# Two fused transformer blocks on one core: state-free delta steps moved ahead, state-space half first in the output projection, layer norms per token tile

## The chip, the cores and the metric

One core of one Trainium2 chip. The metric is the device time in microseconds (us) of one execution of the whole program; lower is better. PE is the matrix engine (TensorE), DVE the vector engine, ACT the scalar engine, POOL GpSimd, SP the engine that issues the weight transfers.

## What is computed

Everything is float32, with 256 tokens of width 1024. Block 1 is attention, convolution and memory attention, then a mixture of 32 experts. Block 2 runs two recurrences, a state-space scan (SSD) and a gated delta rule (GDN), over 256 context tokens and then over the 256 latent tokens, in both directions and in chunks of 64, of which the kernel takes two at a time. The change touches the GDN scan and what comes after it:

```python
def gdn_step(s, inp):                       # per chunk; u, w from a triangular solve
    u_c, w_c, qk_c, qg_c, kd_c, dec_c = inp # these don't depend on the state s
    v_new = u_c - einsum("bhlk,bhkv->bhlv", w_c, s)
    o = einsum("bhlk,bhkv->bhlv", qg_c, s) + einsum("bhls,bhsv->bhlv", qk_c, v_new)
    s = s * dec_c[..., None, None] + einsum("bhlk,bhlv->bhkv", kd_c, v_new)
...
y = rms_norm(y_ssd * silu(z)) * norm_w_ssd
o = rms_norm(o_gdn) * norm_w_gdn * silu(gate)
mixed = concatenate([y, o], -1)                            # 256 x 2048
x = layer_norm(ALPHA * x + g1 * (mixed @ w_out), ln1_g, ln1_b)
h = x * (1 + sc2) + sh2
x = layer_norm(ALPHA * x + g2 * ((silu(h @ w_ffn_gate) * (h @ w_ffn_up)) @ w_ffn_down), ln2_g, ln2_b)
```

g1, sh2, sc2 and g2 are rows of a modulation product, silu(c) @ w_ada + b_ada; the FFN is 2816 wide.

## The kernel before

Each engine's program is written out by hand, and engines wait for each other by semaphores alone. Products go to eight PSUM banks of 128x512; `TileOrder` (L69) hands the banks out in program order (MAIN is 0 to 5, THREE 5 to 7), and a product that opens a bank waits until the engine that reads it has drained the bank's last tile. SP streams the weights in a fixed order through a ring of six 1 MB slots.

The delta rule is cut into phases. `delta_phases` (L109) gives their order, and `gdn_pe` (L580), `gdn_act` (L923), `gdn_dve` (L1147) and `gdn_pool` (L1485) each do their engine's part of a phase and yield its name. There are eight steps: 0 to 3 over the context, whose phases are dealt out between the experts by `mixed_schedule` (L139) from costs in `context_phases` (L121), and 4 to 7 over the latents, one after the other with nothing around them. The phases of a step:
- "rows": PE turns the keys (two tiles of 4 transposes), spreads the decay sums (L551 on), ACT copies them out and POOL masks.
- "gram": PE multiplies keys by keys (gKK) and for latents keys by queries (gQK), L591. DVE makes the masked matrix A from gKK (L1177), copies its 16x16 diagonal blocks (L1184), multiplies them into "spread" (L1191, which gives spread_ready), and then applies the mask to gQK (L1196).
- "rep": PE multiplies blk16 by spread (gRep, four products of 128x512, L614); ACT copies the four tiles (L952); POOL solves the 16x16 blocks in 15 dependent steps of two instructions (L1525, L1526) on Y and then expands Y into XT (eight instructions of 128x128, L1528), which gives XT_ready.
- "kS", "M", "u", "M2", "t", "w", "x", "v", "out": the products with the state and the solve. "M" waits for XT_ready (L621); "w" also holds go1, the queries by the state, whose scaling DVE does at L1207; "out" gives the outputs (go2, added by DVE at L1216) and the next state (gS, L1222 and L1223).
The phases rows, gram and rep of step m+1 lie between those of step m; for the first step of a sequence they stand ahead. Around the latent steps, at the phases in `MOD_PHASES` (L504), PE does a piece of the modulation product: `mod_sum` (L767, row at L771) and `mod_part` (L760, L2068), with ACT copying a part and DVE adding at L1349 (`modulate`).

`second_block_pe` (L696) runs the block in order: channels, SSD steps 4 to 7 (one loop, in each two gate tiles, L1921, and then the inner product, L754), the latent delta steps, 16+16 transposes of the rows y and o (L1915), the output projection `long_product("w2", ...)` (L806) from four weight units, 16 transposes of the normed rows h_ffn, then gate and up products of the FFN (tiles of 256 channels by 256 tokens, "fg0" the first), and `long_product("fd", ...)`. On DVE, `gated_y` (L1352) forms and squares the y rows, `normed_y` (L1362) scales a quarter of them, `o_squares` (L1376) measures an o tile; `residual` (L1423) adds a product tile to x and sums rows; `layer_norm` (L1434) works over both token tiles in one go: centre and square both, one root, then scale and shift each, with `modulated` (L1448) for h_ffn. POOL multiplies x by ALPHA once h_ffn is there.

```python
for phase in ("kS", "M", "rows", "u", "M2", "gram", "t", "w", "rep", "x", "v", "out"):
...
MOD_PHASES = ["gram 4", "rep 4", "kS 4", "v 4", "v 5", "v 6", "u 7", "w 7", "v 7"]
```

## Time and profile before

| what | value |
|---|---|
| median of 3 runs | 1818.27 us (1816.91, 1818.27, 1820.97) |
| the profiled execution, its own time | 1816.53 us |
| its span (first to last instruction) | 1814.8 us |
| PE busy | 1586.8 us, 87% |
| DVE busy | 666.5 us, 37% |
| ACT busy | 382.7 us, 21% |
| POOL busy | 229.4 us, 13% |
| HBM read | 369.98 MB, 204 GB/s over the span |
| chain that ended last, by engine | PE 69%, DMA 17%, DVE 6%, POOL 3%, ACT 2% |

All times of the trace are microseconds from the start of the span, those marked ns apart. A timeline row reads: start, length of the group from its first start to its last end, engine and line, operation, what it writes and reads with partitions x elements, how many instructions, and in brackets the idle time of the engine before the group and what ended it. PE counts two instructions for one float32 product, and one for a transpose (L1915). The granted clock (PEclk) is a share of full speed: 1.0 is 2.4 GHz and 0.5 is 1.2 GHz.

### The profile page before, as it was taken

How to read it: one execution, taken by the hardware profiler on the slowest of the kernel's cores; microseconds unless marked ns; L12 is line 12 of the kernel's file. 1: busy time of each engine (PE TensorE's matmuls, PEld its weight loads, DVE VectorE, ACT ScalarE, POOL GpSimd, SP SyncE). 2: the span in 40 equal slices, each digit the busy share in tenths (PEclk: the TensorE clock that was granted, in tenths of full speed). 3: DMA queues.
4: the chain of work that ended last, by engine and by line, in shares of the span. 5: the costliest groups of instructions: out<-in, count | busy, mean ns of one | idle time of the engine just before them, and what ended most of it. 6: DMA issues, size and time to landing. Idle time of an engine off the chain costs nothing.

```text
span 1814.8 us, 22881 instructions
## 1 busy us (share of the span) xinstructions
PE 1586.8 (87%) x9344; PEld 1073.8 (59%) x9344; DVE 666.5 (37%) x1395; ACT 382.7 (21%) x830; POOL 229.4 (13%) x423
## 2 busy tenths in 40 slices
PE   7999999998788877798899799899587789699996
PEld 3558555447555554366666488645376664488842
DVE  2207212435333334332343377756455550300003
ACT  1001355013211112233232141322233320100000
POOL 2000000020000000323422100010555500100000
PEclk9999999998988898899999799999799889799998
DMA  7454425741998997999999533412611133144440
GB/s 245 144 174 147 139 93 198 258 141 37 390 391 338 397 353 297 382 393 380 412 378 397 210 140 139 140 48 94 241 47 47 47 140 139 60 172 140 140 157 28
DMA packets 124285, 372.52 MB, mean 205 GB/s; under 512 B 10523, under 2 KB 26517, under 8 KB 107413
## 3 DMA queue, kind: packets, MB, share of 16 engines
q1 hardware_dynamic: 118245, 361.12, 52.9%
q0 software_dynamic: 1568, 8.39, 1.2%
q10 hardware_dynamic: 4368, 1.54, 0.4%
q8 instruction: 76, 1.25, 0.3%
q14 instruction: 28, 0.23, 0.0%
HBM read 369.98 MB, written 1.05 MB: 204 GB/s over the span
## 4 chain that ended last, share of the span: by engine, by line
PE 69%; DMA 17%; DVE 6%; POOL 3%; ACT 2%; issue 2%; SPq 0%; DVEq 0%; ACTq 0%; POOLq 0%
PE psum L1921 49%; DMA ring<-in_w_up 7%; DMA ring<-in_w_down 5%; PE psum L591 5%; DMA ring<-in_w_in 4%; PE psum L1720 3%; PE psum L1915 2%; PE psum L1761 2%; PE psum L1704 1%; PE psum L614 1%; POOL area L1525 1%; PE psum L1742 1%; POOL area L1526 1%; POOL area L1528 1%; PE psum L2038 1%
## 5 line engine op out<-in xcount | busy, mean ns | idle before, releaser
L1921 PE MATMUL psum<-area,ring 128*128 128x256 f32 x1984 | 450.9, 387 | 12.0 <-DMA ring<-in_w_in 11.0
L1921 PE MATMUL psum<-ring,area 128*128 128x512 f32 (+1 forms) x1040 | 451.8, 594 | 8.7 <-DMA ring<-in_w_proj_mem 2.3
L1921 PEld LDWEIGHTS psum<-area,ring 128*128 128x128 f32 x1984 | 381.0, 194 | 70.5 <-DMA ring<-in_w_in 15.2
L1921 PEld LDWEIGHTS psum<-ring,area 128*128 128x128 f32 x1040 | 198.6, 192 | 252.9 <-issue 251.8
L591 PE MATMUL psum<-area 128*128 128x128 f32 x1536 | 194.3, 285 | 43.1 <-POOL area L1528 37.8
L591 PEld LDWEIGHTS psum<-area 128*128 128x128 f32 x1536 | 184.7, 198 | 65.7 <-POOL area L1528 39.3
L1720 PE MATMUL psum<-ring,area 128*32 128x256 f32 x2048 | 135.9, 413 | 49.5 <-DMA ring<-in_w_up 49.5
L2194 ACT ACTIVATE area<-psum 128x512 f32<-128x512 f32 x116 | 66.5, 599 | 458.9 <-PE psum L1921 360.8
L1720 PEld LDWEIGHTS psum<-ring,area 128*32 128x32 f32 x2048 | 70.1, 117 | 103.3 <-issue 74.8
L1915 PE MATMUL psum<-const,area 128*128 128x128 f32 (+1 forms) x544 | 89.7, 297 | 37.7 <-DVE area L1452 14.8
L1915 PEld LDWEIGHTS psum<-const,area 128*128 128x128 f32 (+1 forms) x544 | 70.5, 152 | 71.2 <-issue 20.5
L1117 DVE SCALAR_TENSOR_TENSOR area<-area,cols 128x268 f32<-128x268 f32 (+1 forms) x186 | 91.6, 492 | 6.6
L1742 PE MATMUL psum<-ring,area 128*32 128x256 f32 x1024 | 68.2, 396 | 20.8 <-DMA ring<-in_w_down 20.5
L932 ACT COPY area<-psum 128x512 f32<-128x512 f32 x96 | 54.3, 587 | 100.1 <-PE psum L591 86.3
L1476 POOL TENSOR_TENSOR area<-area 128x1024 f32<-128x1024 f32 x4 | 9.3, 2353 | 498.4 <-DVE area L2316 498.4
L895 ACT COPY area<-psum 128x256 f32<-128x256 f32 x62 | 23.2, 373 | 208.5 <-PE psum L1921 208.5
L1115 DVE TENSOR_SCALAR area<-area,cols 128x268 f32<-128x268 f32 (+1 forms) x62 | 22.1, 356 | 114.3 <-ACT area L895 114.3
L1463 DVE TENSOR_TENSOR area<-psum,area 128x512 f32<-128x512 f32 x11 | 7.6, 692 | 151.2 <-PE psum L1921 151.2
L1742 PEld LDWEIGHTS psum<-ring,area 128*32 128x32 f32 x1024 | 30.6, 112 | 51.1 <-DMA ring<-in_w_down 24.9
L1871 DVE TENSOR_TENSOR area<-psum,area 128x128 f32<-128x128 f32 x32 | 9.3, 290 | 124.7 <-ACT area L1823 124.7
L1426 DVE TENSOR_TENSOR area<-psum,area 128x512 f32<-128x512 f32 x8 | 5.5, 692 | 128.6 <-PE psum L1921 128.6
L1525 POOL TENSOR_TENSOR area<-area 128x120 f32<-128x120 f32 (+14 forms) x120 | 44.7, 373 | 61.1 <-ACT area L952 52.4
(307 smaller groups left out, 1372.1 us busy)
## 6 DMA issues: line engine op xcount, KB each, us to landing
ring<-in_w_gate SPq DMA_DIRECT2D x64, 1024.0 KB, 9.6
ring<-in_w_up SPq DMA_DIRECT2D x64, 1024.0 KB, 11.5
ring<-in_w_down SPq DMA_DIRECT2D x64, 1024.0 KB, 12.2
ring<-in_w_in SPq DMA_DIRECT2D x29, 2048.0 KB, 8.3
ring<-in_w_ada SPq DMA_DIRECT2D x12, 2048.0 KB, 8.1
ring<-in_w_in SPq DMA_DIRECT2D x13, 1024.0 KB, 11.1
ring<-in_w_out SPq DMA_DIRECT2D x6, 2048.0 KB, 7.9
ring<-in_w_ffn_gate SPq DMA_DIRECT2D x5, 2048.0 KB, 9.0
```

The costliest lines, as they stand in the source:

```text
L591: last = nc.tensor.matmul(dst[:, i * P:(i + 1) * P], lhs(4 * h + i), rhs(4 * h + i), start=True, stop=True)
L895: nc.scalar.copy(dst, src).then_inc(drain_of(key), 1)
L932: nc.scalar.copy(b[name][:, 4 * h:4 * h + 4, :], src).then_inc(drain_of((key, m, h)), 1)
L1115: link(v.tensor_scalar(dst, src, w, None, ALU.mult))
L1117: link(v.scalar_tensor_tensor(dst, src, w, dst, ALU.mult, ALU.add))
L1525: link(g.tensor_tensor(tmp[:, 0:n, :], rep[:, left, :, j], Y[:, j:j + 1, :].to_broadcast([P, n, GDN_HEADS]), ALU.mult))
L1720: last = nc.tensor.matmul(wide.dst[CAP * j:CAP * (j + 1), 0:2 * P], hcT[:, q % 2, k, rows], both[:, :, k % 4, j * P:(j + 1) * P], start=k ...
L1742: last = nc.tensor.matmul(dst[CAP * g:CAP * (g + 1), 0:256], actT_e[:, e % 2, CAP * j:CAP * (j + 1)], w[:, j % 2, g * 256:(g + 1) * 256], ...
L1761: nc.tensor.matmul(dst, placeT[:, q, t * P:(t + 1) * P], y_quad[:, q % 2, half * WIDE:(half + 1) * WIDE], start=True, stop=True).then_inc( ...
L1915: last = nc.tensor.transpose(t[0:width, j * P:j * P + rows], src, ident[0:rows, 0:rows])
L1921: last = nc.tensor.matmul(dst, lhs(k), rhs(k), start=first and k == 0, stop=final and k == count - 1)
L2194: nc.scalar.activation(dst, src, func).then_inc(drain_of(key), 1)
```

## The change

- `delta_phases` gets two more phases after "v": "cross" (the gQK products with DVE's L1196, out of "gram") and, after "out", "expand" (the eight expansion instructions of L1528, now on DVE, after it has waited for Y_ready, which POOL gives in the place of XT_ready). go1 and its scaling move from "w" to "x". The five names in STATE_FREE run one step ahead. Both new phases cost 0 in the context planner, so that nothing else of that schedule moves, nor does the order of the weight stream.
- The phases "rows 4", "gram 4" and "rep 4" are taken into the last SSD step: on PE after its state product, between its two gate tiles and ahead of its inner product. In MOD_PHASES "cross 4" and "expand 4" take the places of "gram 4" and "rep 4", so DVE's modulate(4) stands behind "expand 4". POOL does "rows 4" ahead of two transfers that it issues.
- The output projection begins with the state-space half: the y rows are turned in "t 7" and "x 7", `normed_y` runs in "kS 6", "u 6", "M2 6" and "v 6", `normed_o` of tile 1 in "x 7"; the w2 product opens banks 0 to 3, does w20 and w21, turns the o rows in banks 4 and 5 (`turn_o`), and does w22 and w23.
- The layer norms go token tile by token tile (`summed`, `centred`, `normed`). POOL multiplies the rows of gain and shift with those of the modulation ahead of time (ffn_rows), so that h_ffn is written directly; x for the second residual is made by POOL afterwards, in three instructions of 128x1024 per tile. fg0 is done per token tile (128 columns), between the tiles' transposes.

```diff
-    order = [(phase, steps[0]) for phase in ("rows", "gram", "rep")]
+    order = [(phase, steps[0]) for phase in STATE_FREE]
     for m in steps:
-        for phase in ("kS", "M", "rows", "u", "M2", "gram", "t", "w", "rep", "x", "v", "out"):
-            if phase not in ("rows", "gram", "rep"):
+        for phase in ("kS", "M", "rows", "u", "M2", "gram", "t", "w", "rep", "x", "v", "cross", "out", "expand"):
+            if phase not in STATE_FREE:
                 order.append((phase, m))
             elif m + 1 in steps:
                 order.append((phase, m + 1))
@@ -121,7 +122,7 @@
...
+                if phase == "cross":
                     for h in range(2 if side else 0):
                         eight("gQK", h, of("kT"), lambda head: qT[:, head, tok])
...
-                    for h in range(2 if side else 0):
-                        eight("go1", h, lambda head: qT[:, head, tok], lambda head: state[:, head, :])
                 if phase == "x":
                     for h in range(2):
                         wait_drained(pe, ("gw", m, h))
                         eight("gx", h, of("M2T"), of("U"))
+                    for h in range(2 if side else 0):
+                        eight("go1", h, lambda head: qT[:, head, tok], lambda head: state[:, head, :])
...
-                gate_tiles(GATES[2 * i:2 * i + 2])
+                if i == 3:
+                    assert next(delta_steps) == "rows 4"
+                    gate_tiles(GATES[6:7])
+                    assert next(delta_steps) == "gram 4"
+                    gate_tiles(GATES[7:8])
+                    assert next(delta_steps) == "rep 4"
+                else:
+                    gate_tiles(GATES[2 * i:2 * i + 2])
...
+                if phase in ("t 7", "x 7"):
+                    t = ("t 7", "x 7").index(phase)
+                    pe.wait_ge(s["y_ready"], (t + 1) * SSD_G)
+                    turn_rows(0, t)
...
+            def turn_o():
+
+                for t in (1, 0):
+                    pe.wait_ge(s["o_normed"], 2 - t)
+                    turn_rows(1, t)
                 for t in range(NT):
                     for half in range(2):
-                        wait_drained(pe, ("yoT", src, t, half))
-
...
+                banks = [open_tile((key, t, half), FOUR, closes_next=False) for t in range(NT) for half in range(2)]
                 k0 = 0
                 for n, name in enumerate(names):
+                    if middle and n == len(names) // 2:
+                        middle()
...
-            long_product("w2", [f"w2{i}" for i in range(4)], yoT)
-
...
+            first, = unit("fg0")
+            first_banks = [open_tile(("fg", j), FOUR, closes_next=False) for j in range(2)]
...
+                for j in range(2):
+                    for c in range(2):
+                        last = hidden_tiles("fg", 0, first, j, c, t, first_banks[j])
+                    if t == NT - 1:
+                        order.close(("fg", j))
+                        last.then_inc(filled, 1)
...
+                if phase == "expand":
+                    eng.wait_ge(s["Y_ready"], m + 1)
+                    for head in range(GDN_HEADS):
+                        ins = v.tensor_tensor(b["XT"][:, head, :].rearrange("p (g j) -> p g j", j=16),
+                                              b["Y"][:, :, head].unsqueeze(1).to_broadcast([P, 8, 16]),
+                                              blk16.rearrange("p (g j) -> p g j", j=16), ALU.mult)
...
+            def summed(key, gate, ss, gain, bias, dst, signal):
+
+                for half in range(2):
+                    residual(key, 0, half, gate)
+                centred(ss, 0)
+                residual(key, 1, 0, gate)
+                eng.wait_ge(s["norm_rows_ready"], 1)
+                normed(ss, 0, gain, bias, dst[:, 0, :], signal)
+                residual(key, 1, 1, gate)
+                centred(ss, 1)
+                normed(ss, 1, gain, bias, dst[:, 1, :], signal)
 
...
-                    for head in range(GDN_HEADS):
-                        ins = g.tensor_tensor(b["XT"][:, head, :].rearrange("p (g j) -> p g j", j=16),
-                                              Y[:, :, head].unsqueeze(1).to_broadcast([P, 8, 16]),
-                                              blk16.rearrange("p (g j) -> p g j", j=16), ALU.mult)
-                    ins.then_inc(s["XT_ready"], 1)
+                        ins = g.tensor_tensor(Y[:, left, :], Y[:, left, :], tmp[:, 0:n, :], ALU.subtract)
+                        if n > 1:
+                            link(ins)
...
-            for phase in gdn_dve(eng, LATENT, link, spread):
+            for phase in delta_steps:
                 if phase in MOD_PHASES[1:]:
                     modulate(MOD_FIRST + MOD_PHASES.index(phase) - 1)
-                if phase == "rep 4":
-                    gated_y()
+                if phase == "cross 4":
+                    for t in range(NT):
+                        gated_y(t)
+                    root_ask(y_root, 512)
+                if phase == "M 4":
...
-                if phase in ("kS 7", "u 7", "t 7", "w 7"):
-                    n = ("kS 7", "u 7", "t 7", "w 7").index(phase)
+                if phase in ("kS 6", "u 6", "M2 6", "v 6"):
+                    n = ("kS 6", "u 6", "M2 6", "v 6").index(phase)
                     normed_y(n // SSD_G, n % SSD_G)
-
-            eng.wait_ge(s["gate_gain"], NT)
-            root_take(o_root[:, 1, :])
+                if phase == "x 7":
+                    normed_o(1)
...
+            eng.wait_ge(s["norm_in"], 16 * 4)
+            eng.wait_ge(s["mod_drained"], 12 - MOD_FIRST)
+            eng.wait_ge(s["o_normed"], NT)
+            gain, bias = ffn_rows[:, 0, :], ffn_rows[:, 1, :]
+            g.tensor_tensor(gain, norm_rows[:, 0, :], mod_rows[:, 2, :], ALU.mult)
+            link(g.tensor_tensor(bias, norm_rows[:, 1, :], mod_rows[:, 2, :], ALU.mult))
+            g.tensor_tensor(bias, bias, mod_rows[:, 1, :], ALU.add).then_inc(s["norm_rows_ready"], 1)
+            eng.wait_ge(s["norm_rows_ready"], 1)
+            link(g.tensor_scalar(norm_rows[:, 0:2, :], norm_rows[:, 0:2, :], ALPHA, None, ALU.mult))
+            for t in range(NT):
+                eng.wait_ge(s["h_ffn_ready"], t + 1)
+                link(g.tensor_tensor(x[:, t, :], x[:, t, :], stats[:, 6 + t:7 + t].to_broadcast([P, D]), ALU.mult))
+                link(g.tensor_tensor(x[:, t, :], x[:, t, :], norm_rows[:, 0, :], ALU.mult))
+                g.tensor_tensor(x[:, t, :], x[:, t, :], norm_rows[:, 1, :], ALU.add).then_inc(s["x_scaled"], 1)
```

How the instructions of PE move, without the line shift (L591 is L593 afterwards, L614 L617, L771 L782, L2068 L2150, L1915 L1997, L1921 L2003, L754 L765; a count is of program instructions). PE from the last SSD step's state product to the first latent "M", before:

```order
L745 MATMUL psum<-area 128x512 x2
L1921 MATMUL psum<-ring,area 128x512 x16
L754 MATMUL psum<-area 128x64 x16
L1915 MATMUL psum<-const,area 128x128 x16
L591 MATMUL psum<-area 128x128 x16
L2068 MATMUL psum<-ring,area 32x512 x8
L614 MATMUL psum<-area,const 128x512 x4
L771 MATMUL psum<-area 128x512
L2068 MATMUL psum<-ring,area 32x512 x8
L591 MATMUL psum<-area 128x128 x8
L771 MATMUL psum<-area 128x512
L2068 MATMUL psum<-ring,area 32x512 x8
```

and with the change:

```order
L749 MATMUL psum<-area 128x512 x2
L1997 MATMUL psum<-const,area 128x128 x16
L2003 MATMUL psum<-ring,area 128x512 x8
L593 MATMUL psum<-area 128x128 x8
L2003 MATMUL psum<-ring,area 128x512 x8
L617 MATMUL psum<-area,const 128x512 x4
L765 MATMUL psum<-area 128x64 x16
L593 MATMUL psum<-area 128x128 x8
L2150 MATMUL psum<-ring,area 32x512 x8
L782 MATMUL psum<-area 128x512
L2150 MATMUL psum<-ring,area 32x512 x8
L593 MATMUL psum<-area 128x128 x8
```

The products of "rows", "gram" (8 of its 16) and "rep" now stand ahead of the SSD step's inner product, and the two gate tiles lie between them; gQK (8) is behind it. One cycle of a latent delta step on PE, from the q sums on, before:

```order
L778 MATMUL psum<-const,area 128x1 x8
L591 MATMUL psum<-area 128x128 x40
L614 MATMUL psum<-area,const 128x512 x4
L591 MATMUL psum<-area 128x128 x16
L771 MATMUL psum<-area 128x512
L2068 MATMUL psum<-ring,area 32x512 x8
L591 MATMUL psum<-area 128x128 x40
L1915 MATMUL psum<-const,area 128x128 x16
```

and with the change:

```order
L789 MATMUL psum<-const,area 128x1 x8
L593 MATMUL psum<-area 128x128 x24
L617 MATMUL psum<-area,const 128x512 x4
L593 MATMUL psum<-area 128x128 x24
L782 MATMUL psum<-area 128x512
L2150 MATMUL psum<-ring,area 32x512 x8
L593 MATMUL psum<-area 128x128 x48
L1997 MATMUL psum<-const,area 128x128 x16
```

Of the 40 products ahead of the rep product, gQK (8) has moved behind "v" and go1 (8) to "x"; the sum is the same. PE from the end of the last step's "v" to the FFN, before:

```order
L591 MATMUL psum<-area 128x128 x16
L771 MATMUL psum<-area 128x512
L591 MATMUL psum<-area 128x128 x8
L1915 MATMUL psum<-const,area 128x128 x32
L1921 MATMUL psum<-ring,area 128x512 x64
L1915 MATMUL psum<-const,area 128x128 x16
L1921 MATMUL psum<-area,ring 128x256 x352
```

and with the change:

```order
L1997 MATMUL psum<-const,area 128x128 x8
L593 MATMUL psum<-area 128x128 x8
L782 MATMUL psum<-area 128x512
L593 MATMUL psum<-area 128x128 x8
L2003 MATMUL psum<-ring,area 128x512 x32
L1997 MATMUL psum<-const,area 128x128 x16
L2003 MATMUL psum<-ring,area 128x512 x32
L1997 MATMUL psum<-const,area 128x128 x8
L2003 MATMUL psum<-area,ring 128x128 x32
L1997 MATMUL psum<-const,area 128x128 x8
L2003 MATMUL psum<-area,ring 128x128 x32
L2003 MATMUL psum<-area,ring 128x256 x320
```

Half of the 32 transposes of y and o rows stands ahead of go2 (the last L593 x8), the other half in the middle of the projection, and fg0 is 2 x 32 products of 128 columns in the place of 32 of 256.

## Rows read from the trace of the kernel before

**Rows 1.** Windows of PE: stretch, us, PE busy (instructions), PEclk, DMA share, GB/s

```profile
800.00:1000.00 200.00, 179.00 (x1973) 1.00 0.97 394
1300.00:1310.00 10.00, 0.00 (x0) 0.52 0.64 235
1490.00:1495.00 5.00, 4.31 (x5) 0.51 0.00 0
```

**Rows 2.** Timeline of PE, last SSD step to the first latent M

```profile
1254.49 13.90 PE L1921 MATMUL psum<-ring,area 128*128 128x512 f32 x32
...
1283.99 6.74 PE L614 MATMUL psum<-area,const 128*128 128x512 f32 x8 [4.91 <-DVE area L1191]
...
1296.22 1.92 PE L2068 MATMUL psum<-ring,area 128*32 128x512 f32 x16
1312.67 6.10 PE L591 MATMUL psum<-area 128*128 128x128 f32 x32 [14.53 <-POOL area L1528]
```

**Rows 3.** Timeline of POOL, first latent solve

```profile
1292.99 0.88 POOL L1525 TENSOR_TENSOR area<-area 128x120 f32<-128x120 f32 x1 [6.25 <-ACT area L952]
...
1308.81 3.80 POOL L1528 TENSOR_TENSOR area<-area,const 128x128 f32<-128x128 f32 x8
```

**Rows 4.** Timeline of PE, one cycle of the latent scan

```profile
1363.83 1.91 PE L1915 MATMUL psum<-const,area 128*128 128x128 f32 x16
...
1380.58 2.05 PE L591 MATMUL psum<-area 128*128 128x128 f32 x16 [2.29 <-DVE area L1196]
1382.47 3.60 PE L614 MATMUL psum<-area,const 128*128 128x512 f32 x8
...
1405.23 5.91 PE L591 MATMUL psum<-area 128*128 128x128 f32 x32 [7.17 <-POOL area L1528]
```

**Rows 5.** Timeline of DVE, the same cycle

```profile
1372.10 2.16 DVE L1177 SCALAR_TENSOR_TENSOR area<-psum,area 128x128 f32<-128x128 f32 x8 [0.90 <-PE psum L591]
...
1377.63 2.29 DVE L1191 TENSOR_TENSOR area<-area,stats 128x2048 f32<-128x2048 f32 x1
...
1397.22 0.69 DVE L1223 TENSOR_TENSOR area<-psum,area 128x512 f32<-128x512 f32 x1
```

**Rows 6.** Timeline of POOL, the same cycle

```profile
1371.73 2.37 POOL L1582 TENSOR_TENSOR area<-area,gdn_gain 128x1024 f32<-128x1024 f32 x1
...
1388.33 0.49 POOL L1525 TENSOR_TENSOR area<-area 128x120 f32<-128x120 f32 x1 [5.59 <-ACT area L952]
...
1401.37 3.80 POOL L1528 TENSOR_TENSOR area<-area,const 128x128 f32<-128x128 f32 x8
```

**Rows 7.** Source view of DVE's subtraction L1201: ns min/median/max

```profile
L1201 DVE TENSOR_TENSOR area<-area x12: 677/693/1444, 899.8 to 1453.0; 128x512 f32<-128x512 f32 x12
```

**Rows 8.** Timeline of PE, last step to the FFN

```profile
1475.32 1.95 PE L591 MATMUL psum<-area 128*128 128x128 f32 x16
...
1490.69 57.28 PE L1921 MATMUL psum<-ring,area 128*128 128x512 f32 x128 [1.16 <-ACT area L2194]
...
1567.74 155.00 PE L1921 MATMUL psum<-area,ring 128*128 128x256 f32 x704 [0.99 <-ACT area L2194]
```

**Rows 9.** Timeline of DVE, the same stretch

```profile
1478.17 0.69 DVE L1216 TENSOR_TENSOR area<-psum,area 128x512 f32<-128x512 f32 x1
...
1548.08 0.69 DVE L1426 TENSOR_TENSOR area<-psum,area 128x512 f32<-128x512 f32 x1 [2.01 <-PE psum L1921]
...
1554.69 1.28 DVE L1445 SCALAR_TENSOR_TENSOR x<-x,stats,area 128x1024 f32<-128x1024 f32 x1
...
1591.62 0.69 DVE L1463 TENSOR_TENSOR area<-psum,area 128x512 f32<-128x512 f32 x1 [26.90 <-PE psum L1921]
```

**Rows 10.** Timelines of DVE and POOL beside the experts, at context step 0's expansion

```profile
760.47 0.29 DVE L1871 TENSOR_TENSOR area<-psum,area 128x128 f32<-128x128 f32 x1 [8.41 <-ACT area L1823]
...
775.58 0.29 DVE L1871 TENSOR_TENSOR area<-psum,area 128x128 f32<-128x128 f32 x1 [11.76 <-ACT area L1823]
...
771.02 3.81 POOL L1528 TENSOR_TENSOR area<-area,const 128x128 f32<-128x128 f32 x8
```

159 lines of the change are left out of this document (86 added, 73 removed).

## The prediction

> **What bounds the kernel now.** I read four views. The page says which engine carries the chain that ended last: PE with 69% and the weight transfers with 17%. Windows then split the run. From 800 to 1000 us the experts keep the DMA engines at 0.97 [rows 1], and nothing that PE or DVE saves there can be had before the weights land. In the latent delta scan the transfers are idle or wait for room, and at 1300 to 1310 PE does nothing at all at a granted clock of 0.52, so there the bound is a chain of dependent steps over PE, DVE, ACT and POOL. Timelines of that stretch follow the chain: gram product, DVE's spread (L1191), the rep product, ACT's copies, POOL's solve and expansion, the M product [rows 2, 3] for the first step, [rows 4 to 6] for one of three like cycles. The last view is the tail, from the last go2 to the first FFN tiles [rows 8, 9], where PE stands first for transposes and copies, then for the layer norm. The change touches just these three places. I sum against the profiled execution's own time of 1816.53 us; the median of the runs shown is 1.74 above it, and I add that at the end.
>
> **A, the head of the scan.** Today the gate tiles begin at 1254.49 and the first M ends at 1312.67 + 6.10 = 1318.77 [rows 2]. Afterwards PE does, from 1254.5 on: 16 transposes (1.9, L1915 in [rows 4]), a gate tile (13.90 / 2 = 7.0), eight gram products (2.0), a gate tile: 1272.4. DVE needs 1379.92 - 1372.10 = 7.8 us from L1177 to the end of L1191 [rows 5], under the second gate tile; it starts near 1264.5, and with some SSD work between I put the spread at 1273.4. The rep product at full clock takes 3.6 [rows 4] where it took 6.74 after a gap of 4.91 [rows 2]: 1277.0. From its end to the first solve step were 1292.99 - 1290.73 = 2.3 us [rows 2, 3]: 1279.3. The solve took 1308.81 - 1292.99 = 15.8 [rows 3] while DVE formed the y rows, but 1401.37 - 1388.33 = 13.0 [rows 6] with DVE nearly idle; since `gated_y` still runs beside it I take 15.8: 1295.1. The expansion: between 8 x 0.29 = 2.3, DVE's time for a 128x128 multiply [rows 10], and a little over POOL's 3.80 [rows 3]; I take 4.0: 1299.1. Then a new wait: DVE does modulate(4) behind the expansion (0.7), and PE's mod_sum(5) and mod_part ahead of M wait for it. They are a quarter of a rep product and 1.92 [rows 2, 4], 2.8 at full clock and some 4.8 after an idle stretch: M starts at 1304.6 and takes 3.8 warm, 1308.4. **A = -10.4**; with a solve of 13.0 and an expansion of 2.3, -15. What is queued behind the waiting PE is only M itself. The inner SSD products (L754) and gQK, now behind rep, fill the solve's shadow and cost nothing; without that cover gQK alone would cost 2.0. POOL's two transfers are issued one phase later and are wanted only steps later.
>
> **B, three cycles.** The rep product starts at 1382.47, behind go1 and gQK, which waited 2.29 us until 1380.58 for L1196 to free a bank [rows 4]. The spread was ready at 1379.92 [rows 5]. With both moved behind the rep product it starts then: -2.45 in two cycles; in the third, two `normed_y` pieces stand ahead on DVE, so -1.7. From rep to M it was 1405.23 - 1382.47 = 22.8 [rows 4]. Y is ready at 1401.37, 18.9 after rep. DVE must by then be through its "out" additions: they ended at 1397.91 [rows 5], the move of rep adds 2.45 and L1196, now among them, 1.3, so 19.2. The expansion ends between 19.2 + 2.3 = 21.5 and 19.2 + 3.8 = 23.0. I take the upper end, because DVE then runs beside POOL's next multiplications: the 128x512 subtraction L1201, which stands in the same place, took 693 ns in the middle and up to 1444 [rows 7], and POOL's own step of 128x120 took 0.88 beside a working DVE [rows 3] and 0.49 alone [rows 6]. So M comes 0.25 later after rep: **B = -2.45 - 2.45 - 1.7 + 0.75 = -5.85**; if the short expansion holds, about -10.
>
> The Trainium skill ("GPSIMD Engine Reference", the engine selection section) has VectorE 1.96 times as fast as GpSimd at a two-input elementwise instruction; by it the expansion would fall from 3.80 to 1.94 in all four latent steps, and the whole sum would be 7 us lower. No row here shows L1528's form on DVE.
>
> The clock: M after the 7.17 gap took 5.91, and half a gram's worth (x16) takes 2.05 warm [rows 4], so a warm M (4.0) would give 1.9 back; but the gap before rep widens, since go1 and gQK no longer stand in it, from 2.29 [rows 4] toward the 4.91 after which rep took 6.74 [rows 2], which would cost 3.1. I put the two at zero against each other; this is my least certain term.
>
> **C, start of the output projection.** go2 ends at 1475.32 + 1.95 = 1477.3, and w2 starts at 1490.69 [rows 8]. Added ahead of go2: 16 transposes of y rows (1.9) and half a microsecond or so of DVE's normed_o(1) ahead of the "v" subtractions: go2 ends at 1479.8. Bank 0 holds the second go2 half, which DVE drained 1478.86 - 1477.3 = 1.6 after [rows 9]; with L1216 a little behind, 2.1. w2 starts at 1481.9: -8.8. It started cold: 1490 to 1495 show 0.51 and only 5 instructions [rows 1], 2.5 us lost, which a gap of 2.1 need not cost. In its middle stand the 16 transposes of the o rows and a drain, 1.9 + 1.16 (the last idle in [rows 8]) = +3.1. The o rows themselves, five DVE instructions of 1.3 [rows 9] and a root behind go2, are ready long before w20 and w21 end (57.28 / 2 = 28.6). **C = -8.8 - 2.5 + 3.1 = -8.2**.
>
> **D, layer norm and fg0.** Let E be the last w2 fill, 1548.0 [rows 8, 9]. Today DVE's first FFN multiply waits until 1591.62 for one fu tile behind fg0; a tile is 32 instructions of 155.00 / 704 = 0.22, or 7.05 [rows 8], so fg0 ends at 1584.5, E + 36.5. Afterwards tile 0's banks fill 7 us ahead of E (two times 57.28 / 16), so its norm waits for little: h_ffn(0) at E + 1.3. Turning and copying it takes 1.9 (half of L1915's 1.91 and a last wait of 0.99, [rows 4, 8]); 64 instructions of half width, at a little over half of 0.22, take 7.5: E + 10.7. For tile 1 the residual, the centring (two instructions and a root) and the two scalings (1.28 each, [rows 9]) would be done at E + 8.3, hidden behind tile 0's products. But h_ffn_ready(0) releases POOL to three instructions of 128x1024 at 2.37 [rows 6] on x just then. [Rows 7] show DVE held for a POOL instruction, once for as long as its own length; if it is held for all three, h_ffn(1) is at E + 14.5. Then 1.9 + 7.5, and 0.75 for fu0's bank, which waits for the Silu of fg0: E + 24.7. **D = -11.8**; unheld, PE goes straight on at E + 10.7 and D = -15.6. Rows for such long instructions on both engines there are none; I take the held case because the one row that exists shows a hold.
>
> The Trainium skill ("SBUF — State Buffer", who interferes with whom) states that DVE with two SBUF inputs and a GpSimd instruction that reads SBUF contend, and that the loser blocks for the whole instruction; by it D is -11.8 and not -15.6, and [rows 7] agree in direction only.
>
> **At nothing.** The final norm: DVE carries it before and after, with as many instructions on the last tile. The expansion in the context steps: DVE now stands behind its multiply of 760.47 until POOL's solve ends at 771.02, then expands until 773.3 and does two short copies; its next urgent work, the multiply at 775.58, comes 1.5 us later [rows 10]. Steps 1 to 3 stand shorter. If that cover goes, it costs what the third rival says. POOL's premultiplied rows (three of 2.37 and one longer) lie under w2.
>
> **Sum.** -10.4 - 5.85 - 8.2 - 11.8 = -36.2: 1780.3 own time, **1782** against the median.
>
> **Rivals.** (1) No holds, and the clock gives: A -15, B -10, C -8.2, D -15.6, together -49, 1769. For it speaks that a hold is seen in a minority of L1201's twelve; against it, that POOL is always busy where DVE expands. Chance 0.17; the skill's 1.96 belongs here. (2) Gaps cost the clock: rep at half clock in three cycles (+9.3), w2 cold (+2.5), and a slip at one new wait, modulate(4) or the middle of w2: -36.2 + 12 = -24, 1794. For it: every gap of 4.91 or more in [rows 2, 4] was followed by slow products. Chance 0.19. (3) The other side: DVE's standing in order at "expand" beside the experts. Its stand and the expansion are 773.3 - 760.8 = 12.5 us, and with the DMA at 0.97 [rows 1] what the stream loses isn't recovered. If the solve ends over 1.5 us later relative to the next expert multiply than in [rows 10], the loss begins; in full it is 4 x 12.5 = 50, 1832. The margin speaks against: chance 0.04. (4) Reordering hides nothing, since another wait ends each stretch at the old time: within 0.2%, 0.02. The forecast has 0.58.
>
> **Numbers.** 0.2% is 3.6 us, about what a measurement of this kernel can tell from no change. Faster 0.58 + 0.17 + 0.19 = 0.94, same 0.02, slower 0.04. The range goes a little past rivals 1 and 2, for a further 6 us of unknown clock each way: 1763 to 1800.
>
> **What would show it.** Right: the first M near 1302 to 1305; rep starting as L1191 ends, with M some 23 us later; w2 starting within 3 us of go2, with 3 us of transposes in its middle; fg0 in two halves that end near E + 11 and E + 24, with DVE instructions over 2 us beside POOL's. Wrong: rep rows of 6.7, PEclk near 0.5 in w2's first 5 us, a gap in the expert stretch ended by a DVE line, or fg0's second half straight behind the first.

## The result, and the profile after

The changed kernel took 1786.93 us (median of 4 runs, 1783.96 to 1788.60) against 1819.62 for the kernel before on the same chip: a ratio of 0.982, 95% interval 0.9803 to 0.9838, so 32.7 us or 1.8% faster. 1782 was predicted, with 1763 to 1800 as range. The profiled execution took 1783.96 for a span of 1782.2, which is 32.6 under the span before.

The page: PE's busy time has not changed (1586.8 before), the share of POOL and of the transfers in the chain has fallen from 3% and 17%, PE's and DVE's has risen.

```profile
PE 1586.6 (89%) x9408; PEld 1074.5 (60%) x9408; DVE 693.8 (39%) x1459; ACT 382.4 (21%) x833; POOL 220.1 (12%) x368
...
PE 71%; DMA 15%; DVE 8%; ACT 2%; issue 2%; POOL 1%; SPq 0%; DVEq 0%; ACTq 0%; POOLq 0%
```

PE's timeline from the last SSD step to the first latent M, the counterpart of [rows 2]. The second row is the rep product, which now comes right behind the gate tile and takes 3.60 us, its time at full clock ("warm" below; "cold" is half clock). PE then does what was behind it, and stands 9.33 us for DVE's modulate(4), L1413.

```profile
1255.62 7.11 PE L2003 MATMUL psum<-ring,area 128*128 128x512 f32 x16
...
1271.21 3.60 PE L617 MATMUL psum<-area,const 128*128 128x512 f32 x8
...
1297.02 2.04 PE L782 MATMUL psum<-area 128*128 128x512 f32 x2 [9.33 <-DVE area L1413]
1298.99 2.41 PE L2150 MATMUL psum<-ring,area 128*32 128x512 f32 x16
1301.33 3.84 PE L593 MATMUL psum<-area 128*128 128x128 f32 x32
```

The second cycle of the scan on PE, as [rows 4]: M, rep, next M. There is no wait for a bank ahead of rep any more, but one of 3.45 for the spread, and rep runs at about half clock. M again follows idle time and takes over 6 us.

```profile
1342.70 6.27 PE L593 MATMUL psum<-area 128*128 128x128 f32 x32 [3.77 <-DVE area L1253]
...
1364.93 5.35 PE L617 MATMUL psum<-area,const 128*128 128x512 f32 x8 [3.45 <-DVE area L1243]
...
1389.46 6.75 PE L593 MATMUL psum<-area 128*128 128x128 f32 x32 [3.76 <-DVE area L1253]
```

The expansion, once POOL's L1528 with 3.80 [rows 6], is DVE's L1253. These are DVE's row in the first cycle and POOL's beside it: eight instructions in 3.90, no less than on POOL, and POOL's multiplications for kv start in the same moment.

```profile
1338.75 3.90 DVE L1253 TENSOR_TENSOR area<-area,const 128x128 f32<-128x128 f32 x8
```

```profile
1338.68 2.08 POOL L1576 TENSOR_TENSOR area<-area 128x512 f32<-128x512 f32 x2
```

Narrower windows take the two rows apart. DVE's first and second instruction took 1.12 us each, one beside each of POOL's two, which had started a little earlier; the other six took 1.80 together, 0.30 each.

```profile
1338.75 1.12 DVE L1253 TENSOR_TENSOR area<-area,const 128x128 f32<-128x128 f32 x1
...
1339.80 1.12 DVE L1253 TENSOR_TENSOR area<-area,const 128x128 f32<-128x128 f32 x1
...
1340.85 1.80 DVE L1253 TENSOR_TENSOR area<-area,const 128x128 f32<-128x128 f32 x6
```

```profile
1338.68 1.04 POOL L1576 TENSOR_TENSOR area<-area 128x512 f32<-128x512 f32 x1
...
1339.67 1.08 POOL L1576 TENSOR_TENSOR area<-area 128x512 f32<-128x512 f32 x1
```

PE's tail, as [rows 8]: go2, w2 in two halves with the turning of the o rows between, then fg0 in two halves behind two sets of transposes.

```profile
1462.67 2.05 PE L593 MATMUL psum<-area 128*128 128x128 f32 x16 [0.69 <-DVE area L1264]
1466.88 29.40 PE L2003 MATMUL psum<-ring,area 128*128 128x512 f32 x64 [2.16 <-DVE area L1276]
...
1499.35 27.70 PE L2003 MATMUL psum<-ring,area 128*128 128x512 f32 x64 [0.78 <-ACT area L2276]
...
1530.47 7.38 PE L2003 MATMUL psum<-area,ring 128*128 128x128 f32 x64 [0.83 <-ACT area L2276]
1540.23 1.09 PE L1997 MATMUL psum<-const,area 128*128 128x128 f32 x8 [2.38 <-DVE area L1514]
1542.15 9.01 PE L2003 MATMUL psum<-area,ring 128*128 128x128 f32 x64 [0.83 <-ACT area L2276]
```

DVE in the layer norm of tile 1, and POOL's rescaling of tile 0 beside it. L1506 took 0.75 for tile 0 a little earlier, and L2410 1.23.

```profile
1528.95 1.95 DVE L1497 CUSTOM_DVE_ANT_0 x<-x,area 128x512 f32<-128x512 f32 x1
...
1531.20 2.47 DVE L1506 TENSOR_SCALAR x<-x,stats 128x1024 f32<-128x1024 f32 x1
1533.71 3.26 DVE L2410 CUSTOM_DVE_ANT_0 area<-x 128x1024 f32<-128x1024 f32 x1
```

```profile
1528.47 1.89 POOL L1672 TENSOR_TENSOR x<-x,stats 128x1024 f32<-128x1024 f32 x1 [42.35 <-DVE area L1514]
1530.44 2.68 POOL L1673 TENSOR_TENSOR x<-x,area 128x1024 f32<-128x1024 f32 x1
1533.20 2.68 POOL L1674 TENSOR_TENSOR x<-x,area 128x1024 f32<-128x1024 f32 x1
```

The DVE instructions end 0.54, 0.55 and 1.09 us behind the POOL instruction beside them, about their own length when nothing is in the way (0.69, 0.75, 1.23): each stands for as long as the POOL instruction runs and then does its own work.

**Where the 32.6 us came from.** I cut each trace at six marks that all kernels share: the start of the last SSD step's state product (L745, afterwards L749), the end of the first latent M, the start of the last M, the start of w2, its end, and the end of fg0 (before, where fg0 and the next tile stand in one row, just ahead of ACT's taking up fg0's last tile at 1584.65). All times are in us; the first column is when the first mark comes.

| kernel | start | to end of first M | to last M | to w2 | w2 | to end of fg0 | from start to fg0 |
|---|---|---|---|---|---|---|---|
| before | 1252.8 | 66.0 | 131.9 | 40.1 | 57.3 | 36.5 | 331.7 |
| changed | 1250.4 | 54.7 | 129.5 | 32.3 | 60.2 | 24.1 | 300.7 |
| e1_no_hoist | 1251.9 | 67.9 | 128.1 | 31.5 | 58.5 | 22.5 | 308.5 |
| e2_cross_back | 1251.3 | 54.7 | 137.7 | 31.6 | 58.5 | 25.1 | 307.6 |
| e3_w2_back | 1256.1 | 54.8 | 128.4 | 40.0 | 57.2 | 22.5 | 302.8 |
| e4_rescale_late | 1260.6 | 56.4 | 130.4 | 32.6 | 60.2 | 19.9 | 299.5 |
| e5_modulate_early | 1245.2 | 52.2 | 128.3 | 31.5 | 58.5 | 22.5 | 292.9 |
| e6_expand_pool | 1250.9 | 51.5 | 128.4 | 32.7 | 60.2 | 22.5 | 295.2 |
| e7_kv_after_expand | 1252.7 | 54.0 | 124.4 | 31.3 | 60.2 | 24.1 | 294.1 |
| e8_normed_o_late | 1258.6 | 54.8 | 129.5 | 31.2 | 58.5 | 23.9 | 297.8 |
| e9_fill | 1254.2 | 54.7 | 122.5 | 29.7 | 58.5 | 25.1 | 290.5 |
| e10_four | 1256.6 | 50.7 | 124.4 | 30.2 | 60.2 | 19.9 | 285.3 |
| e11_four_fill | 1255.9 | 48.8 | 119.7 | 28.6 | 58.5 | 19.9 | 275.5 |
| e12_fg0_whole | 1266.8 | 54.8 | 129.6 | 32.2 | 60.2 | 31.3 | 308.1 |

From the end of fg0 to the end of the span every changed kernel took 231.0 to 231.7 (230.3 before). What varies from run to run is the start, from 1245 to 1267, in the part of the program with the experts that most of these edits don't touch; total times are therefore read beside the stretches, never alone. Of the 32.6 us, 2.3 are that start, 11.3 the head, 2.4 the cycles, 7.8 less 2.9 the start and length of w2, 12.4 the norm and fg0, and 0.7 are lost at the end. The 2.3 of the start lie well within its spread and are chance.

### The profile page after: what moved, and what is told of

Same layout as the page of the kernel before. It is cut to its first block, busy times and chain, and to the rows that moved or that the text cites. A ratio compares the mean times of both kernels' runs of the same rounds, so it can differ in the third digit from the quotient of the medians.

```text
span 1782.2 us, 23021 instructions
## 1 busy us (share of the span) xinstructions
PE 1586.6 (89%) x9408; PEld 1074.5 (60%) x9408; DVE 693.8 (39%) x1459; ACT 382.4 (21%) x833; POOL 220.1 (12%) x368
## 4 chain that ended last, share of the span: by engine, by line
PE 71%; DMA 15%; DVE 8%; ACT 2%; issue 2%; POOL 1%; SPq 0%; DVEq 0%; ACTq 0%; POOLq 0%
PE psum L2003 49%; DMA ring<-in_w_up 7%; PE psum L593 6%; PE psum L1802 5%; DMA ring<-in_w_down 4%; DMA ring<-in_w_in 3%; PE psum L1997 2%; PE psum L617 2%; PE psum L1843 1%; PE psum L1786 1%; PE psum L1824 1%; PE psum L2150 1%; PE psum L2120 1%; DVE area L1253 1%; POOL area L1595 1%
## 5 line engine op out<-in xcount | busy, mean ns | idle before, releaser
L2003 PE MATMUL psum<-ring,area 128*128 128x512 f32 (+1 forms) x1040 | 451.1, 593 | 10.9 <-DMA ring<-in_w_in 2.5
L2003 PE MATMUL psum<-area,ring 128*128 128x256 f32 (+1 forms) x2048 | 450.8, 380 | 9.9 <-DMA ring<-in_w_in 7.5
L2003 PEld LDWEIGHTS psum<-area,ring 128*128 128x128 f32 x2048 | 384.1, 195 | 66.2 <-DMA ring<-in_w_in 12.7
L2003 PEld LDWEIGHTS psum<-ring,area 128*128 128x128 f32 x1040 | 198.5, 193 | 252.4 <-issue 250.5
L593 PE MATMUL psum<-area 128*128 128x128 f32 x1536 | 195.9, 287 | 16.6 <-DVE area L1253 13.4
L593 PEld LDWEIGHTS psum<-area 128*128 128x128 f32 x1536 | 186.6, 201 | 39.2 <-issue 20.2
L1997 PE MATMUL psum<-const,area 128*128 128x128 f32 (+1 forms) x544 | 85.4, 284 | 22.5 <-DVE area L1331 5.6
L1997 PEld LDWEIGHTS psum<-const,area 128*128 128x128 f32 (+1 forms) x544 | 66.4, 145 | 56.8 <-issue 24.3
L1824 PEld LDWEIGHTS psum<-ring,area 128*32 128x32 f32 x1024 | 30.2, 111 | 56.7 <-DMA ring<-in_w_down 27.7
L1595 POOL TENSOR_TENSOR area<-area 128x120 f32<-128x120 f32 (+14 forms) x120 | 44.6, 372 | 52.2 <-ACT area L994 43.4
```

The costliest lines, as they stand in the source:

```text
L593: last = nc.tensor.matmul(dst[:, i * P:(i + 1) * P], lhs(4 * h + i), rhs(4 * h + i), start=True, stop=True)
L1595: link(g.tensor_tensor(tmp[:, 0:n, :], rep[:, left, :, j], Y[:, j:j + 1, :].to_broadcast([P, n, GDN_HEADS]), ALU.mult))
L1824: last = nc.tensor.matmul(dst[CAP * g:CAP * (g + 1), 0:256], actT_e[:, e % 2, CAP * j:CAP * (j + 1)], w[:, j % 2, g * 256:(g + 1) * 256], ...
L1997: last = nc.tensor.transpose(t[0:width, j * P:j * P + rows], src, ident[0:rows, 0:rows])
L2003: last = nc.tensor.matmul(dst, lhs(k), rhs(k), start=first and k == 0, stop=final and k == count - 1)
```

## The experiments

Each kernel is the changed one with the edit shown. Totals are medians, with the kernel before on the same chip.

### One part undone at a time

**e1_no_hoist.** PE, ACT, DVE and POOL begin with the delta steps behind the SSD loop again.

```diff
-                if i == 3:
-                    assert next(delta_steps) == "rows 4"
-                    gate_tiles(GATES[6:7])
-                    assert next(delta_steps) == "gram 4"
-                    gate_tiles(GATES[7:8])
-                    assert next(delta_steps) == "rep 4"
-                else:
-                    gate_tiles(GATES[2 * i:2 * i + 2])
+                gate_tiles(GATES[2 * i:2 * i + 2])
```

> The changed kernel with only the head of the scan undone: rows, gram and rep of step 4 stand behind the last SSD step again. My theory (each of the four parts carries its own share, A = -11.3 by the trace of the changed kernel, from the last SSD state product to the end of the first M): this run is 11 us slower than the changed kernel, about 21 us under the kernel before, and the stretch from L749 to the end of the first M is 66 us again where it was 54.7. Rival (the solve only slides and another wait takes the place): within 3 us of the changed kernel.

Measured: 1796.34 against 1821.59, ratio 0.9868 (0.9837 to 0.9899). The head takes 67.9 us in place of 54.7, so the hoist is worth 13.2, more than 66.0 - 54.7 = 11.3, because the new wait for modulate(4), which the kernel before doesn't have, stays in. PE's idle row shows it: 12.89 us ahead of mod_sum, ended by DVE.

```profile
1283.11 5.99 PE L617 MATMUL psum<-area,const 128*128 128x512 f32 x8 [8.55 <-DVE area L1234]
...
1311.29 2.04 PE L775 MATMUL psum<-area 128*128 128x512 f32 x2 [12.89 <-DVE area L1401]
...
1315.98 3.84 PE L593 MATMUL psum<-area 128*128 128x128 f32 x32
```

The totals' ratios are 0.9868 and 0.982, which makes the run 8.7 us slower than the changed kernel where 11 were expected. The rival is out: the solve didn't just slide.

**e2_cross_back.** The gQK products are back in gram, go1 back in w, for steps 5 to 7.

```diff
-                if phase == "cross":
+                if (phase, m) == ("cross", 4) or phase == "gram" and m > 4:
                     for h in range(2 if side else 0):
                         eight("gQK", h, of("kT"), lambda head: qT[:, head, tok])
...
-                if phase == "x" and side:
+                if phase == "w" and side:
                     for h, heads in halves:
                         v.tensor_tensor(o_tmp[h], four("go1", h), spread(cum_exp[1][:, d, t, 16 + 4 * h:20 + 4 * h], 4, P), ALU.mult)\
```

> The changed kernel with only part B undone for steps 5 to 7: the gQK products and L1249 stand in gram again, go1 and its scaling in w. By the prediction's terms 5.9 us slower than the changed kernel. By the trace of the changed kernel, in which cycles 2 and 3 are no shorter than before, 2.4 slower. Rival (the wider gap before the rep product costs all that B gives, by the clock): rep takes 3.6 to 3.7 in every cycle again where the second took 5.35, and the run is within 1 us of the changed kernel or faster.

Measured: 1791.37 against 1821.59, ratio 0.983 (0.9803 to 0.9858). In the total no difference from the changed kernel can be told. In the trace neither number of mine held: the cycles took 137.7, 8.3 longer than in the changed kernel, and 5.9 longer than before. The windows of PE between the end of the first M and the start of the last, from the kernel before, the changed one and this one, in that order, part the waits from the clock:

```profile
1318.77:1450.63 131.86, 103.25 (x782) 0.92 0.14 49
```

```profile
1305.17:1434.62 129.45, 108.11 (x784) 0.92 0.17 60
```

```profile
1306.00:1443.72 137.72, 107.66 (x783) 0.89 0.16 56
```

The same 782 to 784 instructions kept PE busy for 103.3 us before and for 108 in both others. PE stood idle for 28.6, 21.3 and 30.1. So the move takes 7.3 to 8.7 us of waiting away, and in the trace before the same instructions took 4.9 less. The mean granted clock doesn't show this, it is 0.92 both before and in the changed kernel: what differs is what PE did while it was low. These are the sums over the parts of the two stretches in which the granted clock was 0.50, before (three parts, from 1355, 1403 and 1444 us) and in the changed kernel (five, from 1341, 1365, 1389, 1406 and 1433):

```profile
sum 20.55, PE 7.54; mean PE 2.51
```

```profile
sum 21.96, PE 18.05; mean PE 3.61
```

Before, PE worked for 7.5 of 20.6 us of half clock, afterwards for 18.1 of 22.0; half of the difference, 5.3, is what work at half clock in the place of full clock adds. It lies in four rows: M of the second cycle (6.27 for 5.33) and of the third (6.75 for 5.91), rep of the second (5.35 for 3.60), and 32 instructions of the third cycle behind an idle time of 2.15 (5.47 for 3.86). In this run the two gQK rows behind idle times of 2.27 and 2.63 took 3.60 and 3.52; the one in [rows 4], behind 2.29, took 2.05. The same wait has either outcome.

**e3_w2_back.** The rows y and o are turned in one go behind the last go2, and the w2 product has no middle; normed_y and normed_o stand where they did before.

```diff
-                if phase in ("t 7", "x 7"):
-                    t = ("t 7", "x 7").index(phase)
-                    pe.wait_ge(s["y_ready"], (t + 1) * SSD_G)
-                    turn_rows(0, t)
...
+            pe.wait_ge(s["y_ready"], NT * SSD_G)
+            for t in range(NT):
+                turn_rows(0, t)
+            turn_o()
...
-            long_product("w2", [f"w2{i}" for i in range(4)], yoT, turn_o)
+            long_product("w2", [f"w2{i}" for i in range(4)], yoT)
```

> The changed kernel with only part C undone: 32 transposes in a row behind the last go2, normed_y in step 7, and w2 without its middle. By the prediction 8.2 us slower than the changed kernel; by the changed kernel's trace (w2 starts 7.8 earlier, lasts 2.9 longer) 4.9 slower. Rival (the start of w2 is worth nothing, since the weight stream or the norm rows end that stretch): within 1.5 us of the changed kernel.

Measured: 1789.24 against 1821.59, ratio 0.9816 (0.978 to 0.9852). In the total no difference can be told; in the trace w2 starts 7.7 later and is 3.0 shorter, 4.7 net, as expected. PE's row of the wait is back, together with the slow transposes:

```profile
1473.70 1.97 PE L1996 MATMUL psum<-const,area 128*128 128x128 f32 x8 [6.36 <-DVE area L1445]
...
1479.24 57.17 PE L2002 MATMUL psum<-ring,area 128*128 128x512 f32 x128 [0.73 <-ACT area L2275]
```

**e12_fg0_whole.** fg0 is one piece behind the transposes of both tiles.

```diff
+            for t in range(NT):
                 for half in range(2):
                     wait_drained(pe, ("h_ffnT", t, half))
-                for j in range(2):
-                    for c in range(2):
-                        last = hidden_tiles("fg", 0, first, j, c, t, first_banks[j])
+            for j in range(2):
+                for c in range(2):
+                    last = hidden_tiles("fg", 0, first, j, c, None, first_banks[j])
```

> The changed kernel, but fg0 is done in one piece (256 columns) behind the transposes of both token tiles. The norm still goes tile by tile. By the changed kernel's trace tile 1's copies end 15.1 after w2's last product, and 14.1 of products follow: fg0 ends 29 after it where it ended 24.1, so 5 us slower. So of D's 12.4 about 5 would be fg0's halves and 7 the norm's order. Rival (PE's stand is set by the norm alone and the halves cost PE what they save, 2 x 7.4 against 14.1): within 1.5 us.

Measured: 1797.28 against 1822.08, ratio 0.985 (0.9823 to 0.9878). In the total the difference can hardly be told. In the trace fg0 ends 31.3 behind w2 and not 24.1: the halves are worth 7.2, of which 1.3 is fg0 itself, 15.43 at a lower clock behind the long idle time where 14.1 was reckoned. That leaves 36.5 - 31.3 = 5.2 of D for the norm's order and the clock: fg0 before took 16.7, 1.3 more than here.

### Single waits and the hold

**e4_rescale_late.**

```diff
+            eng.wait_ge(s["h_ffn_ready"], NT)
             for t in range(NT):
-                eng.wait_ge(s["h_ffn_ready"], t + 1)
                 link(g.tensor_tensor(x[:, t, :], x[:, t, :], stats[:, 6 + t:7 + t].to_broadcast([P, D]), ALU.mult))
```

> The changed kernel, but POOL starts its rescaling of x only when both token tiles of h_ffn are there. If DVE is held by POOL's three long instructions (DVE L1497, L1506 and L2410 took 1.95, 2.47 and 3.26 beside them), these fall to 0.69, 0.75 and 1.23, h_ffn of tile 1 comes 5 us earlier, and fg0 ends earlier by 3 to 4 us, since PE is busy with tile 0's products until about 11 us after w2's end: 3 to 4 us faster. Rival (those DVE instructions are slow for another reason, such as DVE's own PSUM or DMA traffic): durations stay, and the run is within 1 us of the changed kernel.

Measured: 1785.30 against 1821.59, ratio 0.9784 (0.9743 to 0.9825), which overlaps with the changed kernel's; the last stretch took 19.9 in place of 24.1. The three DVE instructions, with POOL idle beside them:

```profile
1542.13 0.69 DVE L1497 CUSTOM_DVE_ANT_0 x<-x,area 128x512 f32<-128x512 f32 x1
...
1543.12 0.75 DVE L1506 TENSOR_SCALAR x<-x,stats 128x1024 f32<-128x1024 f32 x1
1543.91 1.23 DVE L2410 CUSTOM_DVE_ANT_0 area<-x 128x1024 f32<-128x1024 f32 x1
```

The rival is out; the hold is POOL's. Of the 4.2, 2.6 is waiting (the 2.38 ahead of the transposes is gone) and 1.6 that fg0's second half ran in 7.38 and not 9.01.

**e5_modulate_early.**

```diff
-                if phase in MOD_PHASES[1:]:
+                if phase in MOD_PHASES[2:]:
                     modulate(MOD_FIRST + MOD_PHASES.index(phase) - 1)
                 if phase == "cross 4":
                     for t in range(NT):
                         gated_y(t)
                     root_ask(y_root, 512)
+                    modulate(MOD_FIRST)
```

> The changed kernel, but DVE does modulate(4) behind cross 4, where it stands idle, and not behind expand 4. By the prediction's term for the new wait (PE's mod_sum(5) and mod_part ahead of the first M stand until DVE is through the expansion), the first M starts right at the expansion's end, 5.0 us earlier; a cold M then gives 2.3 back by the trace of the first M before (6.10 for 3.84): the stretch from L749 to the end of the first M falls from 54.7 to about 52. Rival (M's start is set by the expansion alone, and the modulation pieces only fill the gap): the stretch stays within 0.5 us of 54.7.

Measured: 1782.98 against 1817.60, ratio 0.9814 (0.9785 to 0.9843). The head takes 52.2. M starts right at the expansion's end, 45.9 behind the first mark where it was 50.9, and takes 6.28 where it took 3.84: both halves of the expectation, to 0.2 us.

```profile
1291.11 6.28 PE L593 MATMUL psum<-area 128*128 128x128 f32 x32 [5.79 <-DVE area L1253]
```

**e6_expand_pool.** POOL expands Y behind its solve; DVE's phase expand is empty.

```diff
-                    ins.then_inc(s["Y_ready"], 1)
+                    for head in range(GDN_HEADS):
+                        ins = g.tensor_tensor(b["XT"][:, head, :].rearrange("p (g j) -> p g j", j=16),
...
+                    ins.then_inc(s["XT_ready"], 1)
```

> The changed kernel with the expansion of Y to XT on POOL again, right behind the solve. My theory (the eight instructions take 3.90 on DVE against 3.80 on POOL, and DVE gets to them as Y is ready): from rep's start to M's start 22.9 us as before, within 0.5 us in each latent step, and the whole within 1 us of the changed kernel. Rival (the move to the faster engine is what carries the gain of the scan, 1.96 times as fast by the Trainium skill's GPSIMD Engine Reference): 1.9 us slower in each latent step, 7 in all.

Measured: 1778.88 against 1817.60, ratio 0.9794 (0.9763 to 0.9825), so if anything faster than the changed kernel. From the end of rep to M's start it took 19.12, 19.13 and 19.45 in the three cycles; in the changed kernel 19.18, 19.18 and 19.50, before 19.16. The move of the expansion is worth nothing in the scan. In the first step it costs 3.3 (54.7 against 51.5), through the wait that e5 takes away, since with the expansion on POOL modulate(4) finds DVE free.

**e7_kv_after_expand.**

```diff
                     for h, heads, dims in halves:
                         if m == 4:
                             wait_filled(eng, ("y_inner", 7, 1))
+                        if side:
+                            eng.wait_ge(s["XT_ready"], m + 1)
```

> The changed kernel, but POOL's two 128x512 multiplications for kv (L1576) wait for XT_ready in the latent steps, and no longer start beside DVE's expansion. If DVE's first expansion instruction, 1128 ns where the others take 373, is held by POOL, it falls to 373 and M starts 0.75 us earlier in each of four steps, 3 us in all; the products with r behind M are not late, since kv and r are done 3 us after M's start. If the others are held as well, up to 1.8 a step. Rival (the first one pays for something else, such as the wake-up from the semaphore): 1128 stays, and the run is the same or up to 2 us a step slower by late r.

Measured: 1780.37 against 1817.60, ratio 0.9803 (0.9774 to 0.9831). DVE's expansion, and its subtraction for the products behind M (L1261), which now waits for POOL's multiplications:

```profile
1340.26 2.40 DVE L1253 TENSOR_TENSOR area<-area,const 128x128 f32<-128x128 f32 x8
1343.89 2.04 DVE L1261 TENSOR_TENSOR area<-area 128x512 f32<-128x512 f32 x2 [1.22 <-POOL area L1578]
```

2.40 where it was 3.90. The 1.5 were not the first instruction's 0.75 alone, nor a loss of all eight: by the rows above it was the first two, 1.12 each for 0.38. M comes 1.5 earlier behind rep in each cycle (17.69, 17.70, 18.04), and the subtraction, though it now waits for POOL, is ready in time. The cycles take 5.0 us less.

The Trainium skill ("GPSIMD Engine Reference", elementwise side-by-side cycle accounting) has VectorE 1.96 times as fast at an addition of two inputs; its engine selection section, which the prediction names, says about twice. Here the ratio is 3.80 / 2.40 = 1.6 with POOL quiet and 3.80 / 3.90 = 0.97 beside POOL's own work; the measurement decides.

**e8_normed_o_late.**

```diff
-                if phase == "x 7":
-                    normed_o(1)
-
+            normed_o(1)
             for h in range(2):
                 wait_drained(eng, ("go2", 7, h))
             o_squares(0)
```

> The changed kernel, but DVE does normed_o(1) behind the last go2 additions and not in x 7, where its two 128x1024 multiplications of 1.22 stand ahead of the last subtractions (L1264). These and then go2 and w2 come earlier: the stretch from the last M's start to w2's start falls from 32.3 by 1.3 to 1.7. The o rows of tile 1 are turned 27 us later, so nothing waits for them. Rival (go2 waits for the drain behind gv and not for DVE's queue): the stretch stays.

Measured: 1785.67 against 1817.60, ratio 0.9824 (0.9788 to 0.986). The stretch fell by 1.1, a little under the 1.3 to 1.7 expected; PE's wait ahead of go2 (0.69) is gone. In the total the edit can't be told.

### The clock, and all together

**e9_fill.** PE repeats a product of two constants into the bank that it is about to fill, while it would stand.

```diff
+                def warm(tile, n):
+
+                    dst = open_tile(tile)
+                    for _ in range(n):
+                        nc.tensor.matmul(dst[:, 0:P], blk16, ident, start=True, stop=True)
+                    return dst
...
                 if phase == "rep":
+                    first = warm(("gRep", m, 0), {5: 5, 6: 13, 7: 1}.get(m, 0))
                     pe.wait_ge(s["spread_ready"], m + 1)
...
                 if phase == "M":
+                    first = warm(("gM", m, 0), {5: 14, 6: 14, 7: 22}.get(m, 0))
                     pe.wait_ge(s["XT_ready"], m + 1)
```

> The changed kernel with extra PE products into the bank about to be used (128x128, 0.23 us each at full clock), where PE stands idle: 14, 14 and 22 ahead of M in steps 5 to 7, and 5, 13 and 1 ahead of rep; their results are overwritten. If the slow M products (6.27, 6.75, 6.3) and the slow rep of step 6 (5.35) are the clock after the idle time ahead of them, they fall to 3.8 and 3.7: from the end of the first M to w2's start 129.45 + 32.26 = 161.7 falls by 8 to 9 us. Rival (they are slow for another reason, or the extra products come in the way of the real ones): M stays over 5, or the stretch falls by under 2.

Measured: 1775.09 against 1822.08, ratio 0.9733 (0.9706 to 0.9759), 16 us under the changed kernel by the ratios (0.0087 of 1822), or 10 to 22 by their intervals. The two stretches show 161.7 - 152.2 = 9.5, a little over the 8 to 9 expected; for the rest of the 16 nothing in the trace speaks but the spread of the first part. PE's second cycle, which the rows of the changed kernel above show at half clock:

```profile
1346.45 3.84 PE L600 MATMUL psum<-area 128*128 128x128 f32 x32 [0.64 <-DVE area L1262]
...
1362.64 3.07 PE L593 MATMUL psum<-const 128*128 128x128 f32 x26
1366.26 3.70 PE L625 MATMUL psum<-area,const 128*128 128x512 f32 x8 [0.56 <-DVE area L1252]
...
1389.12 3.84 PE L600 MATMUL psum<-area 128*128 128x128 f32 x32 [0.62 <-DVE area L1262]
```

M took 6.27 and 6.75 there and rep 5.35. Over the windows the granted clock is 0.99 for the cycles and 1.00 from the last M to w2, where both were 0.92. One slow row is left, 5.46 for 32 instructions behind an idle time of 2.15 that nothing fills. The slow products are the clock, and the clock follows PE's idle time.

**e10_four.** The edits of e4, e5, e7 and e8 together.

> The changed kernel with four edits together: POOL's rescaling of x after both tiles, modulate(4) behind cross 4, kv after the expansion, normed_o(1) behind the last go2. One by one their stretches fell by 2.6 (waits only), 2.6, 6.0 (waits 4.5 to 5) and 1.1. If they are independent, from L749 to the end of fg0 it takes 300.7 - 12 = 289 us, of which 1 to 3 lie in the clock's chance, and the kernel is 12 us faster than the changed one. Rival (they share waits): under 8 together.

Measured: 1774.68 against 1822.08, ratio 0.9728 (0.9702 to 0.9754). From the first mark to fg0 285.3, 15.4 less than in the changed kernel where 12 were expected; 19.9 for the last stretch, 50.7 for the head, about what the single edits gave. The rival, under 8 together, is out.

**e11_four_fill.** The four edits and the extra products (22, 8, 8, 16 ahead of M; 5, 13, 1 ahead of rep).

> The four edits and extra PE products ahead of M (22, 8, 8, 16 in steps 4 to 7) and rep (5, 13, 1) together. By the clock theory M takes 3.8 in all four steps and rep 3.7: 8 to 10 us less than with the four edits alone from L749 to w2's start. Rival: no difference beyond 2 us.

Measured: 1764.40 (median of 6, 1755.58 to 1771.24) against 1822.08, ratio 0.9679 (0.9651 to 0.9708). From the first mark to w2 it took 197.2 against 205.3 in e10, 8.1 less. M took 3.74 to 3.84 throughout; step 7's rep still took 5.40 behind an idle time of 1.85 which the single extra product doesn't fill. This is the fastest kernel of the study, 3.2% under the kernel before.

## Why the prediction was right, and where its terms were off

The direction, the size (36.2 forecast, 32.7 measured) and the four places were right. The size was a little lucky: the four terms together gave 31.0 for 36.2, and the 2.3 by which the last SSD step happened to start earlier made up for part of that. By its steps:

- **A**, -10.4 forecast, -11.3 measured. The rep product came warm at 3.60, the first M at 1301.3 with a start 2.3 earlier than before. The term for the wait on modulate(4) was right: e5 shows that it cost 5.0, of which the clock gave 2.4 back. The expansion took 3.90, as I had put it (4.0). The forecast didn't draw the conclusion, that the position of one 0.7 us instruction undoes a fifth of A.
- **B**, -5.85 forecast, -2.4 measured: the largest miss. The waits went somewhat better than reckoned, 7.3 us less idle time. "I put the two at zero against each other", the clock, was the step that failed: rep at 5.35 in the second cycle, slower M products and one slow row in the third cycle made PE's busy time 4.9 us longer for the same instructions. The step gave M back 1.9 for a shorter wait; the idle time ahead of M did shrink, from 7.2 to 3.8, as gQK and go1 went behind rep, but M got slower (6.27 and 6.75 for 5.33 and 5.91). e2 shows that the loss is chance in part: with the old order PE was busy just as long, in other rows.
- **C**, -8.2 forecast, -4.9 measured. w2 started 7.8 earlier for 8.8, since normed_o(1) held DVE's queue for 2.4 and not half a microsecond (without it there, e8 starts w2 1.1 earlier). The 3.1 for the middle was 3.07. The -2.5 for a warm start failed twice over. The cold start had cost only 57.28 - 2 x 27.70 = 1.9, and in the profiled run it stayed, at 1.7 (29.40 for 27.70), behind an idle time of 2.16. Of the twelve kernels with that idle time (2.0 to 2.2; e3 has 0.73) six profiles show the first half warm (e1, e2, e5, e8, e9, e11) and, with the changed kernel's own, six cold (e4, e6, e7, e10, e12).
- **D**, -11.8 forecast, -12.4 measured. fg0's halves ended 10.8 and 24.1 behind w2, for 10.7 and 24.7. The hold by POOL, on which I had only the one row of L1201, is shown by e4: h_ffn of tile 1 came 5.0 us late by it (6.2 reckoned). The Trainium skill's rule ("SBUF — State Buffer", who interferes with whom), that the loser blocks for the whole instruction, agrees with all three pairs of rows, and with the two expansion instructions of 1.12.
- **At nothing.** The experts' part: the expansion of step 0 began at 773.03 and took 3.94, not 2.3, so the margin of 1.5 was used up. DVE's next expert multiply came at 777.90, 0.3 behind the ACT result that it waits for (777.33 + 0.28). Nothing was lost behind it that the trace shows: PE's waits from 755 to 1010 us sum to 31.0 where they were 32.2, and the start of the last SSD step lies within its run-to-run spread. Rival 3 was nearer than its 0.04 suggests, but its price begins only beyond this. The end of the kernel took 0.7 longer, where 0 was forecast.
- **Rivals.** The first's "no holds" is what e4 and e7 build by other means; the second's clock is what happened in part, about 5 of its 12 us. The sum lies between the forecast and the second.

Left open: why the same idle time of 2.0 to 2.3 us is followed by a slow product in one run and not in another. The totals of e2 to e8 and of e12 can't be told from the changed kernel's, or hardly, over the spread of the first part: their intervals overlap with its 0.9803 to 0.9838. For them the stretches of one trace each speak alone, and what these show of the clock can fall otherwise in the next execution. The totals of e9, e10 and e11 stand clear of it, that of e1 all but.
